# Two more quarters of the query weights loaded into idle gather slots, and two heads routed ahead of the experts

## What is computed

```
q      = h @ peer_wq[i]                     # 1024 x 2048: 8 heads, 2 halves of 128 each
scores = q_half . peer_keys[i][head][half]  # 128 scores per half
top 16 of each half -> 16 x 16 sums -> top 16 pairs: expert = 128 * a + b, gate = softmax
out    = sum over 8 heads x 16 experts of  gate * gelu(h . peer_u[i][expert]) * peer_v[i][expert]
```

## Time and profile before

| | |
|---|---|
| median of 3 runs | 2195.55 us (2194.63 to 2203.05) |
| the profiled execution | 2196.84 us, span 2195.0 us |
| TensorE's mean granted clock | 0.943 |
| PE busy | 1816.2 us (83%) |
| DVE busy | 1466.8 us (67%) |
| ACT busy | 897.5 us (41%) |
| POOL busy | 618.9 us (28%) |
| DMA | 723.76 MB, mean 330 GB/s |

### The profile page before, as it was taken

The page is one execution under the profiler, slowest core; times in us unless marked ns, Lnnn a source line. Parts: engine busy times, 40 slices in busy tenths (PEclk is TensorE's granted clock), DMA queues, the critical chain, the costliest instruction groups (busy, mean ns, idle before and its releaser), DMA issues.

```text
span 2195.0 us, 21985 instructions
## 1 busy us (share of the span) xinstructions
PE 1816.2 (83%) x7101; PEld 1091.2 (50%) x7101; DVE 1466.8 (67%) x3029; ACT 897.5 (41%) x2357; POOL 618.9 (28%) x567
## 2 busy tenths in 40 slices
PE   4888999889978688888678787996798888877786
PEld 3757998788867344443323233354344443333222
DVE  6766956857776666767567767516666668677754
ACT  3446433524463333434334445312433344344433
POOL 1160000000000344434244343103354345443441
PEclk9889989989998899999899999998999899999999
DMA  9654758545563799999899999746899999999996
GB/s 367 265 198 145 262 196 306 177 171 211 202 220 116 316 371 418 418 421 421 338 402 421 421 421 421 319 172 256 362 416 419 419 421 421 421 421 421 421 422 251
DMA packets 114690, 723.76 MB, mean 330 GB/s; under 512 B 11504, under 2 KB 13344, under 8 KB 34064
## 3 DMA queue, kind: packets, MB, share of 16 engines
q0 software_dynamic: 74864, 540.30, 59.6%
q1 hardware_dynamic: 39712, 182.07, 22.7%
HBM read 721.24 MB, written 1.08 MB: 329 GB/s over the span
## 4 chain that ended last, share of the span: by engine, by line
PE 36%; DMA 31%; DVE 20%; ACT 6%; issue 5%; POOL 2%; SPq 0%; DVEq 0%; ACTq 0%; POOLq 0%
DMA X<-in_k_uv,EI 15%; PE PS L2129 14%; DMA Z<-in_k_uv,EI 9%; DMA W<-in_peer_wq 5%; PE PS L2106 5%; DVE junk L1809 4%; PE PS L1822 3%; PE PS L1823 3%; PE PS L1824 3%; DVE ACC L1429 3%; DVE WL L1445 3%; PE PS L1915 2%; ACT WH L999 1%; DMA W<-in_ada_w 1%; PE PS L2182 1%
## 5 line engine op out<-in xcount | busy, mean ns | idle before, releaser
L2129 PE MATMUL PS<-X,dg 128*128 128x512 f32 x1372 | 673.1, 626 | 176.2 <-ACT dg L999 175.4
L1809 DVE CUSTOM_DVE_ANT_0 junk<-H,X 128x1024 f32<-128x1024 f32 x343 | 419.6, 1223 | 254.0 <-DMA X<-in_k_uv,EI 247.0
L990 POOL DMA_INDIRECT X<-in_k_uv,EI x343 | 376.1, 1097 | 623.2 <-PE PS L2129 328.8
L2129 PEld LDWEIGHTS PS<-X,dg 128*128 128x128 f32 x1372 | 251.2, 195 | 553.3 <-ACT dg L999 345.6
L999 ACT ACTIVATE CF<-DOT 128x1 f32<-128x1 f32 x512 | 102.3, 200 | 588.7 <-DVE DOT L1809 588.2
L2129 PE MATMUL PS<-Z,dg 128*128 128x512 f32 x504 | 246.7, 622 | 38.3 <-ACT dg L999 38.2
L1809 DVE CUSTOM_DVE_ANT_0 junk<-H,Z 128x1024 f32<-128x1024 f32 x126 | 154.1, 1223 | 89.9 <-DMA Z<-in_k_uv,EI 86.7
L999 ACT ACTIVATE dg<-CP,CG 128x128 f32<-128x128 f32 x512 | 205.5, 401 | 17.3 <-PE PS L2129 0.6
L2129 PEld LDWEIGHTS PS<-Z,dg 128*128 128x128 f32 x504 | 92.6, 195 | 175.3 <-ACT dg L999 100.4
L1822 PE MATMUL PS<-XH,WH 128*128 128x256 f32 x592 | 176.2, 298 | 2.3 <-ACT XH L999 1.2
L990 POOL DMA_INDIRECT Z<-in_k_uv,EI x126 | 136.3, 1082 | 136.5 <-PE PS L2129 115.8
(11 more groups left out here) (312 smaller groups left out, 2626.8 us busy)
## 6 DMA issues: line engine op xcount, KB each, us to landing
W<-in_ada_w SPq DMA_DIRECT2D x56, 1024.0 KB, 5.1
Y<-in_ada_w SPq DMA_DIRECT2D x16, 1024.0 KB, 5.9
W<-in_k_win SPq DMA_DIRECT2D x16, 1024.0 KB, 5.1
W<-in_peer_wq SPq DMA_DIRECT2D x16, 1024.0 KB, 16.6
W<-in_k_ffi SPq DMA_DIRECT2D x13, 1024.0 KB, 5.4
Y<-in_k_ffi SPq DMA_DIRECT2D x9, 1024.0 KB, 4.9
W<-in_ffn_w_out SPq DMA_DIRECT2D x8, 1024.0 KB, 5.7
W<-in_ab_w_out SPq DMA_DIRECT2D x6, 1024.0 KB, 5.1
```

The lines of the kernel that those rows point to most:

```text
L990: e.indirect_dma_start(out=WS[k][:, :], out_offset=None, in_=I[f"k_uv{ly}"][:, :], in_offset=bass.IndirectOffsetOnAxis(ap=EI[t][:, j:j + 1 ...
L1809: e.tensor_tensor_reduce(junk, H[:, t, :], d[:, 0:D], 1.0, 0.0, ALU.mult, ALU.add, DOT[:, j:j + 1]).then_inc(v_dot, 1)
L2129: p = e.matmul(PS[:, 2 * t + q, :], dgb[n % 4][:, :], d[:, D + q * 512:D + (q + 1) * 512], start=(j == 0), stop=(j == 127))
```

## The change

Four things are done, and all arithmetic stays as it is.

- The second and third quarter of the query weights (`ldq ly 2` to `ldq ly 5`, 4 MB) are loaded before the layer's experts, into four slots of the gather ring (`EARLY`): X4 to X7 in layer 0, ahead of the first quarter; Z1, Z2, W2 and X0 in layer 1, behind it. Such a slot is closed to gathers until 8 gathers after the last matmuls on it, so a layer begins with 8 gather slots. The fourth quarter is loaded into W0 and W1 right after the first one's matmuls.
- Heads 0 and 1 of tile 0 are both routed before the first dot. The matmuls for head 1 go ahead of all tails. `h` of tile 0 stands between the two routes on DVE, `h` of tile 1 behind them.
- In tile 0 of layer 0 the list puts in one more step of `others` after every fourth expert, so tile 1's heads are routed sooner. An assertion demands that the head of the expert 13 places on is routed.
- Gathers take the slot that has been free longest instead of strict rotation. The pooling weights' slots change: `ldp 2` and `ldp 3`, which went to W2 and X3, go to X3 and Z0.

```
+EARLY = {0: [7, 8, 9, 10], 1: [14, 15, 2, 3]}
...
     P("sc", 0)
+    for i in range(2, 6):
+        P("ldq", 0, i)
...
     def keys_part(ly, s4):
-        if s4:
-            P("ldq", ly, 2 * s4)
-            P("ldq", ly, 2 * s4 + 1)
...
+        first, second = route(ly, 0, 0), route(ly, 0, 1)
+        for i in range(2):
+            yield from chunk(i, 0, 128)
+        next(first)
+        P("tt", ly, 1)
+        next(first)
+        for i in range(2):
+            yield from chunk(i, 128, 256)
+            next(first)
+        yield from chunk(2, 0, 256)
+        yield from first
+        yield from chunk(3, 0, 256)
+        P("h", ly, 0)
+        P("ldq", ly, 6)
+        P("ldq", ly, 7)
+        yield from second
+        P("h", ly, 1)
+        ready.add((ly, "h"))
         yield
...
     def others(ly):
         for s4 in range(4):
             yield from keys_part(ly, s4)
-            yield from route(ly, 0, 2 * s4 + 1)
+            if s4:
+                yield from route(ly, 0, 2 * s4 + 1)
...
+            ahead = 128 * t + j + 13
+            assert ahead > 255 or (ly, ahead // 128, ahead % 128 // 16) in ready, (ly, t, j)
...
             next(g, None)
+            if ly == 0 and t == 0 and j % 4 == 3:
+                next(g, None)
...
-        P("ldq", ly, 0)
-        P("ldq", ly, 1)
+        if ly == 0:
+            P("ldq", 0, 0)
+            P("ldq", 0, 1)
         P("ldk", ly)
         g = others(ly)
-        while not {(ly, 0, 0), (ly, "h")} <= ready:
+        while (ly, "h") not in ready:
             next(g)
...
                 P("ldp", i)
+            for i in range(6):
+                P("ldq", 1, i)
             P("po")
...
-    rings = {"w": [0, 1, 2, 11, 12], "q": [0, 1], "p": [2, 6, 7, 8, 9, 10], "g": RING}
+    rings = {"w": [0, 1, 2, 11, 12], "q": [0, 1], "p": [6, 13, 7, 9, 10, 8]}
...
+        if kind == "pq" and a[2] == 3 and a[6] == 8:
+            for k in [k for k, what in held.items() if what == tuple(a[:2])]:
+                held[k] = gathers + 8
...
+        if kind == "ga":
+            gathers += 1
+            free = [k for k in RING if k not in held or isinstance(held[k], int) and held[k] <= gathers]
+            k = min(free, key=lambda k: used[k])
+            held.pop(k, None)
+            used[k] = gathers
+        elif kind == "ldq" and 2 <= a[1] < 6:
+            k = EARLY[a[0]][a[1] - 2]
+            held[k] = (a[0], a[1] // 2)
...
+                    elif kind == "ldq":
+                        w.wait_ge(p_do, 16)
+                        w.wait_ge(p_gate, 4)
+                        w.wait_ge(v_gx, 4)
```

More of the change, by code:

```diff
@@ L371, in chunk @@
             yield
-        if s4 == 0:
-            for lo in (0, 128):
-                for i in range(2):
-                    yield from chunk(i, lo, lo + 128)
-                if lo == 0:
-                    h00 = route(ly, 0, 0)
-                    next(h00)
-                    P("tt", ly, 1)
-                    yield from h00
-                    P("h", ly, 0)
-                    P("h", ly, 1)
-                    ready.add((ly, "h"))
-        else:
+        if s4:
             for i in range(2):
@@ L388, in keys_part @@
             yield from route(ly, 0, 2 * s4)
-        for i in range(2, 4):
-            yield from chunk(i, 0, 256)
+            for i in range(2, 4):
+                yield from chunk(i, 0, 256)
+            yield
+            return
+        first, second = route(ly, 0, 0), route(ly, 0, 1)
[16 more added lines that the diff above has]
+        ready.add((ly, "h"))
         yield
@@ L516, in tenants @@
     last, count, where = {}, {}, {}
-    rings = {"w": [0, 1, 2, 11, 12], "q": [0, 1], "p": [2, 6, 7, 8, 9, 10], "g": RING}
+    rings = {"w": [0, 1, 2, 11, 12], "q": [0, 1], "p": [6, 13, 7, 9, 10, 8]}
     turn = {k: 0 for k in rings}
+    used, held, gathers = {k: -1 for k in RING}, {}, 0
     for kind, *a in plan:
```

15 lines of the change are left out of this document (8 added, 7 removed).

## The result

The changed kernel takes **2211.24 us** (median of 17 runs, 2202.81 to 2222.64) against 2200.44 for the kernel before (median of 17, one of which took 2847.12 us): ratio **1.0058**, interval 1.0041 to 1.0075. It is slower by half a per cent, where 2160 us was forecast. The profiled execution has a span of 2211.0 us, 16 more than before.

A forecast was written before the change was run, and what follows sets the result against it. The prediction took DMA to bound the expert stages: 20.5 us from bytes and 24 us from holes gained, 8.4 us of costs paid, 36 us net, taking the median of 2195.55 to 2160 us, with a range of 2150 to 2177.

The forecast's parts named there:

- What bounds the kernel: Expert stages: bound by DMA, busy for 0.97 to 0.99 of the time, shortened by fewer bytes and no holes.
- Bytes and holes: Expert stages of both layers: four 1 MB loads fewer a layer gain 20.5 us, closed DMA holes 24 us.
- the hole at the change of tiles: Layer 0, 1073 to 1093 us: largest DMA hole, to close because tile 1's head 0 is routed sooner.
- Start of layer 0: Before layer 0's experts: 4 MB loaded ahead make head 0's scores 1.4 us late, bounds 0 and 4.
- Pooling weights: End of layer 0: 2 MB of pooling loads come between the last gathers, costing 3 us, bounds 0 and 5.1.
- A later first dot: Start of each layer's experts: first dot moves from 730.03 to 737.7 us (plus 1.4), costing 2 us a layer, 0 to 6.
- the slack: Ring of eight gather slots: 19.9 us for eight gathers less 10.2 us for one turn leaves 9.7 us.
- The extra step: Layer 0 up to expert 58: PE needs 2.48 us an expert, DMA 2.49; no cost term of its own.
- the first rival: Layer 0's first 59 experts: PE becomes the bound, needing 160 us, 13 over DMA's pace; 2173 us, within an 18% case.
- The third, starving on eight slots: First gathers of a layer: a fixed landing time of 22.4 us starves the eight-slot ring, 2203 us; chance 4%.
- something else in the chain: Whole kernel: something else in the chain eats most of the gain, 2185 to 2200 us; chance 4%.
- What was to be seen: Changed trace: signs such as gather 16's wait gone and last dot near 1391 us; wrong if holes in first 25 gathers.

The follow-up runs named there:

- `loads_only`: Changed kernel's early query loads and slots only, with one head routed before the first dot and no extra step: 2162.77 us, ratio 0.9858 to the kernel before.
- experiment 10: First dot of each layer made late by 9.8 us of dead DVE work: 2182.98 us on `loads_only`, 2215.72 us on the kernel before.
- experiment 7: Kernel before with two heads routed first, old query loads and slots, no extra step, and the rhythm of `woven`: 2218.67 us.
- `woven`: `one_step` with routes and query matmuls of tile 0's heads 2 to 7 interleaved, at most one half or piece a step: 2182.88 us.
- `one_step`: Changed kernel without the extra step after every fourth expert of layer 0's tile 0, and without the assertion: 2187.07 us.
- `woven_late_pool`: `woven` with pooling loads 2 and 3 moved to the slots that come free last, of gathers 252 and 251: 2176.46 us.
- experiment 8: The run of `woven_late_pool`: pooling loads 2 and 3 of `woven` moved to the slots that come free last, 2176.46 us.
- experiment 1: The run of `one_step`: changed kernel without the extra step, 2187.07 us.
- `loads_fast_steps`: `loads_only` with the extra step after every fourth expert of layer 0's tile 0 put in: 2199.39 us.
- experiment 3: The run of `two_heads_only`: kernel before with two heads routed ahead of the dots, 2198.95 us.
- `before_fast_steps`: Kernel before with only the extra step after every fourth expert of layer 0's tile 0 added: 2210.82 us.
- experiments 3 and 9: The runs of `two_heads_only` (2198.95 us) and `loads_only` (2162.77 us), both without the extra step.
- `ring8_only`: Kernel before with only the gather ring cut to the change's open slots, eight, later ten and twelve: 2197.23 us.
- `two_heads_only`: Kernel before with two heads routed ahead of the dots in both layers, with loads, slots and steps as before: 2198.95 us.
- `loads_late_dot`: `loads_only` with 9.8 us of dead DVE work ahead of each layer's first dot: 2182.98 us.

## Why the prediction was wrong, point by point

**What bounds the kernel** was right for the kernel before: with bytes and holes taken away and little added, `loads_only` gains about what was forecast.

**Bytes and holes, 44.5 us.** Right, as far as the runs can tell them apart. `loads_only` is 34.5 us shorter in the stages; its first dots are 2.9 and 3.2 us later than before, which experiment 10 prices at one to one. That makes 40.6 us, with the pooling loads' term still in it. By tile, 10.1 us of the 34.5 lie in tile 1 of layer 0, the hole at the change of tiles (13.1 by bytes in the sum, 10.6 by share), and 11.1 and 13.3 us in the two tiles 0. Which part of these is bytes and which is the hole at gather 16 wasn't separated: experiment 7, meant for it, brought its own wait.

**Start of layer 0, 1.4 us (0 to 4).** Right. W0 and W1 landed at 707.2 and 709.9 us (706 and 708 said), the keys at 713.2 (713 said), the scores started at 715.80 us (714.1 said), and from `MC` to `EI` it took 23.25 us instead of 20.93: 2.3 us.

**Pooling weights, 3 us (0 to 5.1).** Right in kind and about in size. Timeline of the changed kernel, the last gather of layer 0, `ldp 2`, and the last dots; it answers to the earlier trace rows:

```profile
1400.08 0.94 POOL L1025 DMA_INDIRECT X<-in_k_uv,EI  x1 [1.55 <-PE PS L2164]
...
1402.31 0.37 SPq L930 DMA_DIRECT2D X<-in_pool_w_in  x1
...
1428.75 1.23 DVE L1844 CUSTOM_DVE_ANT_0 junk<-H,X 128x1024 f32<-128x1024 f32 x1 [1.96 <-DMA X<-in_k_uv,EI]
1431.62 1.23 DVE L1844 CUSTOM_DVE_ANT_0 junk<-H,X 128x1024 f32<-128x1024 f32 x1 [1.64 <-DMA X<-in_k_uv,EI]
```

The load goes out 2 us behind the last gather, not before it, and still the last dots are 2.9 us apart and 31.5 us lie between last gather and last dot, as in `woven`; in `one_step` and `woven_late_pool`, where the loads come later, it is 26.2 and 26.3. That is 5 us, and by experiment 8 about 3 net. The place of these loads hangs on the extra step (experiment 1), so these 5 us are also in the 28.3 and 31.1 us below.

**A later first dot, 2 us for each layer (0 to 6).** Wrong: 14.5 to 17.3 us for both (the changed kernel against `loads_fast_steps`, `one_step` against `loads_only`), and beyond the upper bound of 12. Against `loads_only`, the first dots of `one_step` come 8.1 and 9.7 us later, 17.8 in sum, and the stages are 17.3 us longer. In the changed kernel the first dot was said for 739.1 us and started at 745.69: 4.6 of the 6.6 us between are a wait for head 0's exponential, which now stands on ACT behind query copies (`mg` in the waits above), 1.9 the later `EI`. But the delay was foreseen in the main; its price wasn't. The step that failed is the slack: "One turn needs [...] 10.2 us. Slack is 9.7 us." That is a turn once the ring turns. In the first turn nothing comes free until the first tail ends, and the ring is dry as soon as eight gathers and two loads have passed. The prediction had worked that out (25 us from 725.5, up to 750) and called it "Tight, not dry". Experiment 10 shows the bytes already missing from 753 us on at a share of 0.93 to 1.00.

**The extra step, priced at nothing of its own.** This is the larger error, 28.3 to 31.1 us. The prediction added up PE's work for 59 experts, "2.48 us an expert, as much as DMA's 2.49", and put the rest into the slack. The sum was too small by 13 us, and the conclusion was wrong by more: from the first tail to expert 58's (747.96 to 939.75 us) PE was busy for 159.4 us, as the first rival had it (160), but the stretch took 191.8 us, and up to expert 63 a dot came every (946.82 - 745.69) / 63 = 3.19 us. Timeline of DVE in the changed kernel, the first piece of head 2's route:

```profile
768.76 0.30 DVE L1770 MAX8 TV<-PS 128x8 f32<-128x128 f32 x1 [12.20 <-PE PS L2153]
```

PE gets the scores behind its backlog of tails and query halves, and reaches them late; DVE has reached that point of its own list and waits 12.20 us, with all the dots behind it standing; then it does the route, PE is through with its backlog and waits for `dg` (76.4 us in 46 waits in this tile, 58.7 in 36 before). Each of the two is idle while the other works off what is queued, once for every head.

What that costs is seen not in the sum of the waits (experiment 3) but in the time that a head takes. From head 2's `EI` to head 7's it is 173.3 us in the changed kernel, 34.7 us a head for 10.8 experts, where DMA at 420 GB/s needs 2.50 us an expert, 27.0 us. In `loads_only` it is 184.5 us, 36.9 us a head for 13.6 experts, where DMA needs 34.0. So a head with a fifth fewer experts took nearly as long, and the difference stood above DMA's time: 7.7 us a head for 2.9. The two other kernels with the extra step have 35.1 and 36.0 us a head (`loads_fast_steps`, `before_fast_steps`). In the thinner stretch that follows DMA sets the pace again and nothing is caught up: tile 1 took 327.3 us in the changed kernel and 322.8 in `one_step` (the difference is that of the pooling loads). And the step bought nothing, since the hole at the change of tiles is also closed without it (experiments 3 and 9). That the step is the cause, three pairs of runs show. That it acts by this taking of turns is read from the timeline and from the time of a head; no run takes the turns away and leaves the step in. The Trainium skill, "Perfetto Trace Analysis", Roofline, calls a kernel bound by latency (stalls and dependencies) when the utilization of the matmuls and that of HBM are both low. This trace doesn't meet that sign and stands still for dependencies all the same: from 745 to 954 us PE was busy for 81%, and 352 GB/s is 98% of the 358 GB/s that the page counts as full, but 84% of what a full window moved here.

Slots that still hold query weights add to it. A slot is closed until 8 gathers behind the last matmuls in the list, but POOL runs further ahead than that, so the gather waits for PE: 11.99 us in the changed kernel and 12.08 in `loads_fast_steps`, but also 8.53 in `one_step` and 9.34 in `loads_only`. The holes around them miss 12.5 us of transfer in the changed kernel (853 to 873 us) and 6.1 in `one_step` (873 to 893 us). How much of the extra step's price goes through them stays open; they aren't needed for it, since `before_fast_steps`, which has no such slot, loses 26.6 us in tile 0 as well.

**The rivals.** The first, PE as the bound up to expert 58, was nearest: its place and its 160 us of PE were right, "TensorE busy without a break" was not (81%), and its 13 us are less than half. The third, starving on eight slots, had the number nearest to the result (2203 us) and the dry ring, and that is luck: it laid the cost on the time to land, and `ring8_only` shows that eight slots alone cost nothing. None of the rivals had two engines waiting for one another in turn, and the chance for "something else in the chain", 4% at 2185 to 2200, was both too small and too low.

**What was to be seen.** Gather 16's wait for `EI` and the holes at the change of tiles are gone, two query loads stand among the gathers, eight gathers go out before the first wait for a tail, the last dots are 3 us apart: all as said. Of the signs of being wrong one came, the holes in the first 25 gathers: the five windows from 753 to 803 us move 313 to 351 GB/s. The last dot of layer 0 was to start near 1391 us and started at 1431.62; in `loads_only` it started at 1391.34. Layer 1, which has no extra step, was to take 15 us less and took 4.5 less (13.3 in `loads_only`).

## What to carry to other kernels

Where two engines with fixed orders hand work to each other, adding up each one's busy time gives a lower bound and no more: look for the instruction at which one waits behind the other's backlog, and compare the time from one handover to the next with what the stream needs for the items between them. The sum of the waits alone misleads: 72.2 us of them cost little in `two_heads_only`, and 62.2 went with a loss of 28.9 us in `loads_fast_steps`. A list that pulls background work forward can make a stretch in which the stream starves, and the thinner stretch behind it can't give that back once DMA sets the pace. And a change made of several parts should be timed by parts: here one part gained 1.4%, one cost nothing alone and 17 us of the stages together with the first, and two lines cost nearly the whole gain (28.3 to 31.1 us of 34.5).

## What the runs showed of the hardware

The DMA engines' share of busy time hides a short queue. In `loads_late_dot` a window with a share of 0.93 moved 340 GB/s, where one with 1.01 moved 420: the share is 8% lower and the bytes are 19% fewer. In `one_step` a window had 0.95 and 326 GB/s:

```profile
763.00:773.00 10.00, 10.00 (x33) 5.92 (x32) 1.23 (x2) 4.05 (x16) 3.29 (x4) 1.00 0.95 326
```

It goes with few gathers under way: in the changed kernel, 1.8 gathers on average are between issue and landing from 753 to 763 us (share 0.89, 313 GB/s) and 3.8 from 813 to 823 us (1.02, 426 GB/s). So whether a ring is long enough is read from GB/s.

The prediction weighed the per-core HBM limit of about 358 GB/s against the rows. The Trainium skill, "Perfetto Trace Analysis", Roofline, says that a core running alone can go beyond that share, up to about 435 GB/s for its 16 DMA engines together. The traces agree with that: in every kernel here, nine in ten of the windows of 10 us with a share over 1.00 moved 415 GB/s or more, and the fullest 424 to 429. A window at 358 GB/s (`loads_late_dot`, 763 to 773 us) was 15% short of 420.
